# Ten instead of eight of 22 output steps by seven products, with one weight sum formed in DRAM by accumulating transfers

## The chip, the cores and the metric

The kernel runs on one core of one Trainium2 chip. The metric is the device time of one launch in microseconds (us). TensorE (PE) multiplies, VectorE (DVE) and ScalarE (ACT) prepare its operands and read its results, the queue of SyncE (SP) issues the weight loads, and GpSimd (POOL) issues the rest of the transfers through its own, software-driven queue. All transfers share the core's 16 DMA engines.

## What is computed

Two layers of a decoder on 256 tokens of width 2048, all in float32. Each layer is an attention block with a memory branch, followed by a convolutional feed-forward network, which holds most of the work:

```python
def conv_ffn(h, w_in, conv_w, conv_b, w_out):      # h [256, 2048], w_in [2048, 11264]
    u = h @ w_in
    up = jnp.pad(u, ((0, 0), (CONV_WIDTH - 1, 0), (0, 0)))
    c = conv_b
    for j in range(CONV_WIDTH):
        c = c + conv_w[j] * up[:, j:j + s]
    g, val = c[..., :D_FF], c[..., D_FF:]
    return (jax.nn.gelu(g, approximate=True) * val) @ w_out      # w_out [5632, 2048]
...
for layer in range(DEPTH):                          # DEPTH = 2
    mix = mla_mixer(...) if layer == 0 else diff_mixer(...)      # both end in concat(...) @ w_o
    x = x + rms_norm(mix, attn_norm_post)
    f = conv_ffn(rms_norm(x, ffn_norm_pre[layer]), ...)
    x = x + rms_norm(f, ffn_norm_post[layer])
```

The change concerns `@ w_out`, once in each layer.

## The kernel before

**Splitting.** Every float32 operand is held as two float32r parts, hi and lo with hi + lo = value, and a product is three matmuls (hi·hi, hi·lo, lo·hi). A weight block arrives as `w_raw`; ACT copies it to `w_hi` (the "split" of a step, `hi_ready`), DVE subtracts to get `w_lo` (`lo_ready`), then PE uses both (`step_used`). The program is one long row of numbered steps of two 128-row chunks by 512 columns (512 KB): first the memory products (`MEMA`, `MEMB`), the attention products (`QLAT` to `OA`), the feed-forward input `IN0` (176 steps in a loop of 11 turns) and output `OUT0`, then for layer 1 `SKV`, `BQ`, `OB`, `IN1`, `OUT1`. `w_raw`, `w_hi` and `w_lo` are rings of R = 4 slots: the load of a step waits until DVE has finished with the step four before it, and ACT's copy waits until PE has used that step. SP, ACT, DVE and PE each run their own list in order.

**The output stage.** hᵀ (5632 x 256, as `hT_hi`, `hT_lo`) stays on chip; W_out streams by. The 2048 columns are four tiles of 512, taken as two halves of two tiles. One tile has FSTEPS = 22 steps. A *plain* step is 2 chunks x 2 groups of 128 tokens x 3 = 12 matmuls of 512 columns into two PSUM banks. For the first PAIRS = 8 steps of a tile, the two tiles of a half are taken together as a *unit*: the four blocks of W (B11 and B21 of the left tile, B12 and B22 of the right one) and the four of h make a 2 x 2 block product, which is done by the seven products of Winograd's form of Strassen's scheme. That is 7 x 3 = 21 matmuls for what two plain steps do in 24. A unit is four entries of the list: `left` (6 matmuls), `corner` (3), `odd` (6), `even` (6). Three of its products need sums of weight blocks: DVE forms the odd sum (1024 columns, L2439) after `left`, and the even sum (512 columns twice, L2449 and L2452) after `corner`. The sums of h blocks ("forms") are made in the first PAIRS / 2 = 4 turns of the input loop and stay on chip in `s32_*` (in the room of x) and `s4_*`. At the end of a half, five DVE operations ("fold", L2905 to L2909, then L2913) gather the seven banks into tiles.

**The order of entries.** A table sets it by hand (`out_order`): a half has some plain steps first (`LEADS`), then the units with plain steps spread between them, then `REST` = 3 plain steps of the first tile (the fold hides behind them) and `TAILS` of the second. In the units' stretch the hi and lo rings have a fifth slot, `w5_*`, in room that xT has left.

**x and the other transfers.** x leaves for DRAM (`x_kept`) at the start of each input stage and comes back during the output stage, in four pieces of 512 KB (`x_returns`, L704), each after a pair of units of the second half; the fourth goes out when the last unit is done. `gain_o`, `gain_f`, `late_raw` and the memory keys and values (`km_kept`, `vm_kept`) go through POOL's queue as well.

Of the kernel before, what the change touches and what calls it, by code (L numbers as in the profile page):

```python
# [22 lines left out]
P = 128  # L23
# [26 lines left out]
R = 4  # L50
# [7 lines left out]
PAIRS = 8  # L58
# [7 lines left out]
LEADS = (CUT, 5)  # L66
REST, TAILS = 3, (4, 8)


def out_order():  # L70

    entries, raws = [], []

    def plain(tile, k):
        entries.append(("plain", tile, k, len(raws)))
        raws.append((tile, k, "entry", len(entries) - 1))

    def unit(half, p):
        r = len(raws)
        entries.extend((kind, 2 * half, p, r) for kind in ("left", "corner", "odd", "even"))  # L80
        for tile in (2 * half, 2 * half + 1):
            raws.append((tile, p, "unit", half * PAIRS + p))
# [27 lines left out]
WIDE = 100  # L110


def out_slots():

    slots, users, last = [], [], {k: k - R for k in range(R)}
    last[R] = -1
    for e in range(OSTEPS):
        slot = e % R
        turn = e - UNIT_STARTS[0]
        if 0 <= turn < WIDE:  # L120
            turn = turn % (R + 1)
            slot = (UNIT_STARTS[0] + turn - 1) % R if turn else R
        slots.append(slot)
        users.append(last[slot])
        last[slot] = e
    assert all(slots[e] == e % R for e in list(range(CUT)) + list(range(OSTEPS - R, OSTEPS)))
    assert EXTRA % R == 0 and OSTEPS % R == 0
    return slots, users


OUT_SLOTS, OUT_USERS = out_slots()
UNITS = 2 * PAIRS
PAIR_ENDS = [e + 1 for e in range(OUT_ENDS[1], OSTEPS) if OUT_ENTRIES[e][0] == "even"]
# [93 lines left out]
def raw_no(s):  # L227

    if s < OUT0:
        return s  # L230
    if s < SKV:
        return OUT0 + OUT_ENTRIES[s - OUT0][3]
    if s < OUT1:
        return s - EXTRA
    return OUT1 - EXTRA + OUT_ENTRIES[s - OUT1][3]
# [16 lines left out]
def program(nc, x_in, mem_in, positions, inv_freq, w, vec, out):  # L252

    with ExitStack() as ctx:
# [19 lines left out]
        raw_blocks = w_raw[:, :, :].rearrange("p r (a n) -> p (r a) n", a=2)  # L274
# [3 lines left out]
        s32_hi = at("s32_hi", [P, PAIRS // 2, 512], F32R, X0)  # L278
        s32_lo = at("s32_lo", [P, PAIRS // 2, 512], F32R, X0 + 8 * KB)
        s4_hi = at("s4_hi", [P, PAIRS // 2, 256], F32R, KVB0)  # L280
        s4_lo = at("s4_lo", [P, PAIRS // 2, 256], F32R, KVB0 + 4 * KB)
# [108 lines left out]
        def out_slot(e):  # L390


            slot = OUT_SLOTS[e]
            if slot == R:
                return w5_hi[:, :], w5_lo[:, :], w5_sum[:, :]
            return w_hi[:, slot], w_lo[:, slot], w_sum[:, slot]

        def unit_blocks(r):


            left, right = 2 * (r % R), 2 * ((r + 1) % R)
            outer = slice(left, left + 4, 3) if left < right else slice(right + 1, left + 1, 5)
            return (raw_blocks[:, outer, :], raw_blocks[:, left + 1], raw_blocks[:, right],
                    raw_blocks[:, right + 1])

        def odd_columns(r):


            low, high = slice(0, 512), slice(512, 1024)
            return (low, high) if r % R < R - 1 else (high, low)  # L410
# [32 lines left out]
        w_landed = [sem(f"w_landed{k}") for k in range(R)]  # L443
# [69 lines left out]
        odd_sums = sem("odd_sums")  # L513
# [7 lines left out]
        kv_spilled = sem("kv_spilled")  # L521
# [24 lines left out]
        def _(sp):  # L546
# [48 lines left out]
            def out_weights(s_out, name, layer):  # L595

                for r, (j, k, _, _) in enumerate(OUT_RAWS):
                    if r < R:
                        sp.wait_ge(lo_ready, s_out + r - R + 1)
                    elif OUT_RAWS[r - R][2] == "entry":  # L600
                        sp.wait_ge(lo_ready, s_out + OUT_RAWS[r - R][3] + 1)
                    else:
                        sp.wait_ge(unit_sums, layer * UNITS + OUT_RAWS[r - R][3] + 1)
                    sp.dma_start(w_raw[:, r % R, :].rearrange("p (c n) -> p c n", c=2),
                                 view[name][:, 2 * k:2 * k + 2, 512 * j:512 * (j + 1)])\
                        .then_inc(w_landed[r % R], 16)
# [48 lines left out]
        def _(pool):  # L655
# [17 lines left out]

            pool.wait_ge(lam_prod, 1)
            causal_rows(1)
            pool.wait_ge(o_lo, T0_B)
# [22 lines left out]
            def x_returns(s_out):  # L699


                for q in range(4):
                    pool.wait_ge(step_used, s_out + PAIR_ENDS[2 * q + 1])
                    pool.dma_start(x[:, :, 512 * q:512 * (q + 1)],  # L704
                                   x_kept[:, :, 512 * q:512 * (q + 1)]).then_inc(x_back, 16)

# [4 lines left out]
                .then_inc(kv_spilled, 16)  # L711
            pool.wait_ge(step_used, IN0 + 11)
            pool.dma_start(vm_kept, vm_b[:, :, :, :].rearrange("p u h n -> p (u h n)"))\
                .then_inc(kv_spilled, 16)
            gain_rows_of("ffn_post0", gain_f, OUT0)
            x_returns(OUT0)
            pool.wait_ge(step_used, SKV)
            causal_rows(2)
            pool.wait_ge(step_used, SKV + 2 * DSTEPS)
            pool.dma_start(kmT_b[:, :, :].rearrange("p h m -> p (h m)"), km_kept)\  # L720
# [2636 lines left out]
```

## Time and profile before

| | |
|---|---|
| median of 3 runs | 2162.6 us (2160.51 to 2163.26) |
| the profiled execution: its time, its span | 2161.88 us, 2159.7 us |
| PE busy in the span | 2147.9 us (99%) |
| DVE, ACT busy | 1620.6 us (75%), 1247.8 us (58%) |
| DMA | 416.68 MB, 193 GB/s on the mean |
| output stages | about 855 to 1084 us and 1924 to 2152 us from the span's start |

The span is what the profiler recorded of one execution; that execution's own time is 2.2 us longer and within the spread of the three runs. "Busy" counts the time in which an engine runs an instruction. Matmuls overlap, so a matmul's own duration is longer than the distance from one to the next; pace is read from a chain of them, as a stretch of time over their count.

### The profile page before, as it was taken

The numbers are of one execution on the slowest core, as the hardware profiler recorded it, in microseconds if no ns is written. First come the engines' busy times: TensorE is split into PE (matmuls) and PEld (weight loads), VectorE is DVE, ScalarE is ACT, GpSimd is POOL, SyncE is SP. The second block draws the span as 40 slices with busy tenths as digits, with TensorE's granted clock in tenths as the row PEclk, the third lists the DMA queues.
The fourth block names the chain that finished last, engine by engine and source line by source line (L and its number), as shares of the span: only waits on it lengthen the run. The fifth ranks groups of instructions, "written<-read, shape, count | busy, mean of one in ns | idle before, by whom it ended". The sixth has DMA issues, their size and how long they took to land.

```text
span 2159.7 us, 32620 instructions
## 1 busy us (share of the span) xinstructions
PE 2147.9 (99%) x11589; PEld 1861.3 (86%) x11589; DVE 1620.6 (75%) x2280; ACT 1247.8 (58%) x1764; POOL 20.1 (1%) x40
## 2 busy tenths in 40 slices
PE   9999999999999999999999999999999999999998
PEld 8989988888888888888888889888888888888887
DVE  5667756777777777988789877567778776779787
ACT  5755755666555555655565567466665555556554
POOL 0000000000000000000000000000000000000000
PEclk9999999999999999999999999999999999999999
DMA  8566266666656566666657644666655656566575
GB/s 285 177 186 182 92 199 195 209 196 191 188 179 204 181 196 201 197 221 211 223 167 225 198 158 127 194 192 196 196 183 179 201 175 204 178 207 209 195 229 189
DMA packets 204392, 416.68 MB, mean 193 GB/s; under 512 B 13245, under 2 KB 13623, under 8 KB 203535
## 3 DMA queue, kind: packets, MB, share of 16 engines
q1 hardware_dynamic: 200687, 400.29, 58.9%
q0 software_dynamic: 3616, 15.21, 2.0%
q8 instruction: 55, 0.90, 0.2%
q14 instruction: 34, 0.28, 0.0%
HBM read 408.11 MB, written 7.34 MB: 192 GB/s over the span
## 4 chain that ended last, share of the span: by engine, by line
PE 97%; DVE 1%; DMA 1%; ACT 0%; issue 0%; SPq 0%; DVEq 0%; ACTq 0%
PE ps L826 29%; PE ps L780 20%; PE ps L1320 20%; PE ps L834 15%; PE ps L864 4%; PE ps L874 3%; PE ps L1563 1%; PE ps L955 1%; PE ps L1466 0%; PE ps L1085 0%; DMA w_raw<-in_ffn_w_out 0%; PE ps L927 0%; PE ps L1020 0%; PE ps L1091 0%; PE ps L1116 0%; PE ps L1028 0%
## 5 line engine op out<-in xcount | busy, mean ns | idle before, releaser
L2504 DVE TENSOR_TENSOR w_lo<-w_raw,w_hi 128x1024 fp32r<-128x1024 f32 x450 | 541.4, 1221 | 256.1 <-ACT w_hi L1783 252.3
L826 PE MATMUL ps<-xT,w_hi 128*128 128x512 f32 x2752 | 657.6, 391 | 0.0
L1783 ACT ACTIVATE w_hi<-w_raw 128x1024 fp32r<-128x1024 f32 (+1 forms) x466 | 476.8, 1040 | 228.7 <-PE ps L780 85.3
L826 PEld LDWEIGHTS ps<-xT,w_hi 128*128 128x128 f32 x2752 | 505.4, 188 | 98.2 <-issue 0.4
L834 PEld LDWEIGHTS ps<-xT,w_lo 128*128 128x128 f32 x2752 | 353.1, 191 | 13.8 <-DVE w_lo L2504 0.4
L834 PE MATMUL ps<-xT,w_lo 128*128 128x256 f32 x2752 | 358.1, 283 | 0.0
L1320 PE MATMUL ps<-w_hi,hT_hi 128*128 128x512 f32 x576 | 224.4, 390 | 0.5 <-DVE w_lo L2428 0.5
L1320 PE MATMUL ps<-w_lo,hT_hi 128*128 128x512 f32 x576 | 224.1, 389 | 0.0
L1320 PE MATMUL ps<-w_hi,hT_lo 128*128 128x512 f32 x576 | 224.1, 389 | 0.0
L780 PE MATMUL ps<-w_hi,xT 128*128 128x512 f32 x640 | 203.3, 392 | 0.0
L2428 DVE TENSOR_TENSOR w_lo<-w_raw,w_hi 128x1024 fp32r<-128x1024 f32 x126 | 151.0, 1222 | 29.4 <-ACT w_hi L1737 25.3
L1737 ACT ACTIVATE w_hi<-w_raw 128x1024 fp32r<-128x1024 f32 x126 | 131.5, 1058 | 56.6 <-DMA w_raw<-in_ffn_w_out 40.3
L1779 ACT ACTIVATE w_hi<-w_raw,gcol 128x512 fp32r<-128x512 f32 x160 | 106.4, 717 | 62.6 <-PE ps L780 52.7
L780 PEld LDWEIGHTS ps<-w_hi,xT 128*128 128x128 f32 x640 | 120.2, 188 | 24.5
L1320 PEld LDWEIGHTS ps<-w_hi,hT_hi 128*128 128x128 f32 x576 | 108.1, 188 | 23.4 <-DVE w_lo L2428 0.9
L1320 PEld LDWEIGHTS ps<-w_hi,hT_lo 128*128 128x128 f32 x576 | 108.1, 188 | 22.6
L1320 PEld LDWEIGHTS ps<-w_lo,hT_hi 128*128 128x128 f32 x576 | 108.1, 188 | 22.4
L2491 DVE SCALAR_TENSOR_TENSOR w_lo<-w_raw,gcol,w_hi 128x512 fp32r<-128x512 f32 x160 | 111.9, 748 | 20.3 <-ACT w_hi L1779 19.6
L780 PE MATMUL ps<-w_lo,xT 128*128 128x512 f32 x320 | 124.7, 390 | 0.0
L1739 ACT ACTIVATE w_hi<-w_sum 128x1024 fp32r<-128x1024 f32 x64 | 68.0, 1063 | 86.1 <-DVE w_sum L2439 51.9
L780 PE MATMUL ps<-w_hi,xbT_hi 128*128 128x512 f32 x256 | 100.1, 391 | 0.0
L780 PE MATMUL ps<-w_hi,xbT_lo 128*128 128x512 f32 x256 | 99.7, 389 | 0.0
(343 smaller groups left out, 2746.0 us busy)
## 6 DMA issues: line engine op xcount, KB each, us to landing
w_raw<-in_ffn_w_in SPq DMA_DIRECT2D x352, 512.0 KB, 4.2
w_raw<-in_ffn_w_out SPq DMA_DIRECT2D x176, 512.0 KB, 4.8
w_raw<-in_shared_w_kv SPq DMA_DIRECT2D x48, 512.0 KB, 4.4
w_raw<-in_a_w_o SPq DMA_DIRECT2D x32, 512.0 KB, 4.8
w_raw<-in_b_w_in SPq DMA_DIRECT2D x32, 512.0 KB, 4.7
w_raw<-in_b_w_o SPq DMA_DIRECT2D x32, 512.0 KB, 4.3
w_raw<-in_a_w_mem_kv SPq DMA_DIRECT2D x16, 512.0 KB, 6.5
w_raw<-in_b_w_mem_kv SPq DMA_DIRECT2D x16, 512.0 KB, 4.0
```

The lines of the kernel that those rows point to most:

```text
L780: mm = nc.tensor.matmul(dst, st, mv, start=first and q == 0, stop=last and q == len(pairs) - 1, skip_group_check=True)
L826: mm = nc.tensor.matmul(ps[:, base + m4, :].rearrange("p (a n) -> p a n", a=2), w_hi[:, slot, cols], xT[:, :, 2 * k + c, :], start=k == c ...
L834: mm = nc.tensor.matmul(ps[:, base + m4, S:2 * S], w_lo[:, slot, cols], xT_hi[:, 2 * k + c, :], start=False, stop=stop and c == 1, skip_gr ...
L864: mm = nc.tensor.matmul(ps[:, bank, 256 * (h % 2):256 * (h % 2) + S], wk[:, P * h:P * (h + 1)], xk, start=bank not in begun, stop=False, s ...
L1320: mm = nc.tensor.matmul(ps[:, bank, :], st, mv, start=bank not in begun and q == 0, stop=False, skip_group_check=True)
L1737: a = nc.scalar.activation(hi, w_raw[:, r % R, :], ACT.Copy)
L1739: a = nc.scalar.activation(hi, sums_now, ACT.Copy)
L1779: a = nc.scalar.activation(w_hi[:, s % R, cols], w_raw[:, s % R, cols], ACT.Copy, scale=gcol[:, row:row + 1])
L1783: nc.scalar.activation(w_hi[:, s % R, 0:width], w_raw[:, s % R, 0:width], ACT.Copy)\
L2428: nc.vector.tensor_tensor(lo, w_raw[:, r % R, :], hi.bitcast(F32), ALU.subtract)\
L2491: d = nc.vector.scalar_tensor_tensor(out=w_lo[:, s % R, cols], in0=w_raw[:, s % R, cols], scalar=gcol[:, row:row + 1], in1=w_hi[:, s % R, ...
L2504: nc.vector.tensor_tensor(w_lo[:, s % R, :], w_raw[:, s % R, :], w_hi[:, s % R, :].bitcast(F32), ALU.subtract)\
```

## The change

It alters the output stages and what feeds them:

- `PAIRS` goes from 8 to 10, so a half has 10 units and 24 plain steps in place of 8 and 28. `LEADS` is (9, 4), `TAILS` (4, 7).
- The odd sum of a unit is no longer DVE's work. POOL forms it in DRAM (`odd_kept`), for two units at a time in four transfers of 512 KB (`odd_part`): two copies of blocks of W_out, and two transfers that add another block to what lies there (`accum_op`). There are 40 such transfers in a layer. Those of layer 0 go out from `MEMB` on, one in four steps (11), one behind each attention item (16), and two in each turn of the input loop (13); those of layer 1 one in four steps from `SKV` on (26), then in the input loop (14).
- A unit now has three loads: `left` 512 KB, `corner` 256 KB, and `odd` 512 KB from `odd_kept`.
- The forms of h go to DRAM (`s_kept`) in five turns of the input loop, and come back for each unit into one of two buffers (`s_now`, 384 KB a unit), when the unit two before it is done. PE waits for them at `corner`. The room of x thus holds two more raw slots (`x_raw`) and a sixth hi and lo slot (`w6_*`), used in the units' stretch ("turns"), until entry 117.
- x comes back from entry 117 on: four pieces, when 117, 118, 119 and 120 entries are done.

The core of the diff:

```diff
-PAIRS = 8
+PAIRS = 10
...
-LEADS = (CUT, 5)
-REST, TAILS = 3, (4, 8)
+LEADS, REST, TAILS = (CUT, 4), 3, (4, 7)
+EARLY_SUMS, MIDDLE_SUMS = 11, 26
...
+            def odd_part(layer, n):
+                g, part = n // 4, n % 4
+                half, p = 2 * g // PAIRS, 2 * g % PAIRS
+                chunk, tile, a, op = ((0, 0, 0, None), (1, 1, 1, None), (0, 1, 0, ALU.add),
+                                      (0, 1, 1, ALU.add))[part]
+                src = view[f"ffn_w_out{layer}"][:, 2 * p + chunk:2 * p + chunk + 3:2,
+                                                512 * (2 * half + tile):512 * (2 * half + tile + 1)]
+                dst = odd_kept[layer][2 * g:2 * g + 2, :, a, :].rearrange("u p n -> p u n")
+                if op is None:
+                    pool.dma_start(dst, src).then_inc(odd_copied, 16)
+                else:
+                    pool.wait_ge(odd_copied, 32 * (layer * PAIRS + g + 1))
+                    if part == 2 and layer + g > 0:
+                        pool.wait_ge(odd_summed, 32 * (layer * PAIRS + g))
+                    pool.dma_start(dst, src, accum_op=op).then_inc(odd_summed, 16)
...
-            pool.wait_ge(o_lo, T0_B)
+            for n in range(EARLY_SUMS):
+                pool.wait_ge(step_used, MEMB + 4 * (n + 1))
+                odd_part(0, n)
+            for n in range(T0_B):
+                pool.wait_ge(o_lo, n + 1)
+                odd_part(0, EARLY_SUMS + n)
             pool.dma_start(gain_o[:, :], vec["a_post"].partition_broadcast(P))\
                 .then_inc(gain_landed, 16)
...
-                    pool.wait_ge(step_used, s_out + PAIR_ENDS[2 * q + 1])
+                    pool.wait_ge(step_used, s_out + X_FREE + q)
                     pool.dma_start(x[:, :, 512 * q:512 * (q + 1)],
                                    x_kept[:, :, 512 * q:512 * (q + 1)]).then_inc(x_back, 16)
...
+            def forms_return(layer, s_out, no):
+                if no < 2:
+                    pool.wait_ge(s_stored, 32 + 16 * PAIRS * (layer + 1))
+                else:
+                    pool.wait_ge(step_used, s_out + UNIT_DONE[no - 2])
+                pool.dma_start(s_now[:, no % 2], s_kept[layer][no % PAIRS]).then_inc(s_landed[no % 2], 16)
...
                     if kind == "corner":
-                        return s(s4_hi, s4_lo, 0, a, 0)
+                        pe.wait_ge(s_landed[no % 2], 16 * (layer * PAIRS + no // 2 + 1))
+                        return s(2, a, 0)
...
-                if kind == "left":
-                    outer, _, b12, _ = unit_blocks(r)
-                    no = raw_no(s0) + r + 1
-                    dve.wait_ge(w_landed[no % R], 16 * (no // R + 1))
-                    dve.wait_ge(step_used, s0 + OUT_USERS[e + 2] + 1)
-                    nc.vector.tensor_tensor(
-                        out_slot(e + 2)[2].rearrange("p (a n) -> p a n", a=2), outer,
-                        b12.unsqueeze(1).to_broadcast([P, 2, 512]), ALU.add)\
-                        .then_inc(odd_sums, 1)
```

DVE's list at the first units of layer 0. Before, the first unit and the plain step behind it (the names are those of the text, with buffer numbers):

```order
L2428 TENSOR_TENSOR w5_lo_56<-w_raw_51,w5_hi_55 128x1024
L2439 TENSOR_TENSOR w_sum_54<-w_raw_51 128x1024
L2424 TENSOR_TENSOR w_lo_53<-w_raw_51,w_hi_52 128x512
L2449 TENSOR_TENSOR w_sum_54<-w_sum_54,w_raw_51 128x512
L2452 TENSOR_TENSOR w_sum_54<-w_sum_54,w_raw_51 128x512
L2431 TENSOR_TENSOR w_lo_53<-w_sum_54,w_hi_52 128x1024 x2
L2428 TENSOR_TENSOR w_lo_53<-w_raw_51,w_hi_52 128x1024
```

Of the change, the same first unit and the `left` and `corner` of the next:

```order
L2532 TENSOR_TENSOR w5_lo_56<-x_raw_58,w5_hi_55 128x1024
L2514 TENSOR_TENSOR w6_lo_60<-x_raw_58,w6_hi_59 128x512
L2525 TENSOR_TENSOR w_sum_54<-w_raw_51,x_raw_58 128x512
L2528 TENSOR_TENSOR w_sum_54<-w_sum_54,x_raw_58 128x512
L2532 TENSOR_TENSOR w_lo_53<-w_raw_51,w_hi_52 128x1024
L2532 TENSOR_TENSOR w_lo_53<-w_sum_54,w_hi_52 128x1024
L2532 TENSOR_TENSOR w_lo_53<-w_raw_51,w_hi_52 128x1024
L2514 TENSOR_TENSOR w_lo_53<-w_raw_51,w_hi_52 128x512
```

The 1024-column sum is gone, the lo part of `odd` is taken straight from a raw slot, and the second unit follows with no plain step between.

POOL's list from the last accumulating transfer of layer 0 to the end of its output stage. Of the change:

```order
L717 DMA odd_kept<-in_ffn_w_out 128x2x512 x2
L785 DMA s_now<-s_kept 128x768 x2
L738 DMA gain_f<-in_ffn_norm_post 128x2048
L785 DMA s_now<-s_kept 128x768 x18
L754 DMA x<-x_kept 128x2x512 x4
```

Before, this place had two rows:

```order
L688 DMA gain_f<-in_ffn_norm_post 128x2048
L704 DMA x<-x_kept 128x2x512 x4
```

Twenty returns of forms were added ahead of x, on the same queue.

SP's list in the last entries of the output stage of the change (from the odd sum of the last unit but one to the end of layer 1); before, this was an unbroken row of 512 KB loads:

```order
L632 DMA x_raw_58<-odd_kept1 128x1024
L632 DMA w_raw_51<-in_ffn_w_out 128x2x512 x3
L632 DMA w_raw_51<-in_ffn_w_out 128x512
L632 DMA w_raw_51<-odd_kept1 128x1024
L632 DMA w_raw_51<-in_ffn_w_out 128x2x512 x10
```

The `128x512` row is a `corner`, the `odd_kept1` rows are the ready sums; the last ten loads feed the plain steps 118 to 127, on the four slots of `w_raw` alone.

## Rows read from the trace of the kernel before

**Rows 1.** The page: busy time of each engine, share, instructions.

```profile
PE 2147.9 (99%) x11589; PEld 1861.3 (86%) x11589; DVE 1620.6 (75%) x2280; ACT 1247.8 (58%) x1764; POOL 20.1 (1%) x40
```

**Rows 2.** What PE waited for: us in total, times, longest.

```profile
PE ps L864 <- ACT w_hi L1764: 1.3, 1, 1.3
...
PE ps L1320 <- DVE w_lo L2428: 0.5, 1, 0.5
```

**Rows 3.** Chain that ended last: start us, us; layer 0's end, then layer 1's output.

```profile
1054.29 9.12 DMA w_raw<-in_ffn_w_out
...
1069.71 1.14 DVE w_lo L2428
...
1070.90 12.58 PE ps L1320 x54
...
1923.79 228.67 PE ps L1320 x1008
```

**Rows 4.** Windows: start:end, length, busy us (count) by engine, PEclk, DMA share, GB/s.

```profile
core 0: us, PE busy (x) PEld busy (x) DVE busy (x) ACT busy (x) POOL busy (x), PEclk, DMA share, GB/s
376.00:855.00 479.00, 478.99 (x2756) 423.23 (x2755) 355.63 (x433) 274.96 (x322) 2.44 (x4) 1.00 0.62 193
881.00:946.00 65.00, 65.00 (x288) 53.83 (x287) 60.44 (x62) 38.44 (x40) 0.00 (x0) 1.00 0.65 210
```

**Rows 5.** Groups of DVE: line, tiles, shapes, count | busy us, mean ns | idle before.

```profile
L2428 DVE TENSOR_TENSOR w_lo<-w_raw,w_hi 128x1024 fp32r<-128x1024 f32 x126 | 151.0, 1222 | 29.4 <-ACT w_hi L1737 25.3
L2439 DVE TENSOR_TENSOR w_sum<-w_raw 128x1024 f32<-128x1024 f32 x32 | 39.0, 1219 | 4.6 <-PE ps L1320 4.6
L2452 DVE TENSOR_TENSOR w_sum<-w_sum,w_raw 128x512 f32<-128x512 f32 x32 | 22.1, 692 | 1.1
L2449 DVE TENSOR_TENSOR w_sum<-w_sum,w_raw 128x512 f32<-128x512 f32 x32 | 22.0, 688 | 5.3 <-PE ps L1320 5.3
L2424 DVE TENSOR_TENSOR w_lo<-w_raw,w_hi 128x512 fp32r<-128x512 f32 x32 | 21.9, 685 | 0.0
L3135 DVE TENSOR_TENSOR scratch<-scratch 128x256 f32<-128x256 f32 x8 | 3.4, 425 | 0.3
```

**Rows 6.** Loads of weights in the input stage of layer 0, 380 to 850 us.

```profile
L552 SPq DMA_DIRECT2D w_raw<-in_ffn_w_in x164: 372/373/548, 381.7 to 838.1; - x164
...
DMA to landing us min/median/max: 3.4/4.2/7.4
```

**Rows 7.** Loads in the output stage issued from 1054 to 1056 us.

```profile
L604 SPq DMA_DIRECT2D w_raw<-in_ffn_w_out x2: 368/368/368, 1054.3 to 1055.4; - x2
...
DMA to landing us min/median/max: 9.1/9.2/9.3
```

**Rows 8.** Returns of x, the whole trace.

```profile
L704 POOL DMA_DIRECT2D x<-x_kept x8: 704/718/728, 995.9 to 2122.8; - x8
...
DMA to landing us min/median/max: 4.2/6.3/8.8
```

**Rows 9.** Short windows, columns as in rows 4, in which the DMA share is near 1.

```profile
12.00:15.00 3.00, 3.00 (x21) 2.69 (x20) 2.03 (x3) 2.75 (x6) 0.00 (x0) 1.00 1.00 391
...
1056.00:1058.00 2.00, 2.00 (x10) 1.69 (x9) 1.93 (x4) 0.60 (x1) 0.00 (x0) 1.00 0.98 254
...
1062.00:1064.00 2.00, 2.00 (x11) 1.65 (x10) 0.00 (x0) 0.57 (x1) 0.00 (x0) 1.00 0.98 331
...
1076.00:1078.00 2.00, 2.00 (x10) 1.65 (x10) 1.23 (x1) 0.17 (x1) 0.00 (x0) 1.00 1.00 351
```

**Rows 10.** Input stage: ACT's timeline, then two pieces of the chain.

```profile
607.81 1.06 ACT L1783 ACTIVATE w_hi<-w_raw 128x1024 fp32r<-128x1024 f32 x1 [1.70 <-PE ps L834]
...
603.17 3.65 PE ps L826 x16
606.82 1.91 PE ps L834 x16
```

**Rows 11.** POOL's timeline: gain_o, and the last return of x.

```profile
280.44 0.68 POOL L677 DMA_DIRECT2D gain_o<-in_a_attn_norm_post  x1 [215.55 <-DVE xT L2812]
...
1054.41 0.72 POOL L704 DMA_DIRECT2D x<-x_kept  x1 [19.69 <-PE ps L1320]
```

**Rows 12.** Use of gain_o: durations in ns, first and last start.

```profile
L2932 DVE TENSOR_TENSOR y_o<-ps,gain_o x3: 1219/1224/1225, 294.3 to 338.0; 128x1024 f32<-128x1024 f32 x3
```

More of the change, by code:

```diff
@@ L62, with load @@
 FJ = F // 512
-LEADS = (CUT, 5)
-REST, TAILS = 3, (4, 8)
+LEADS, REST, TAILS = (CUT, 4), 3, (4, 7)
+EARLY_SUMS, MIDDLE_SUMS = 11, 26
 def out_order():
     entries, raws = [], []
+    def load(kind, tile, k, e, unit_no=None):
+        raws.append((kind, tile, k, e, unit_no))
+        return len(raws) - 1
     def plain(tile, k):
-        entries.append(("plain", tile, k, len(raws)))
-        raws.append((tile, k, "entry", len(entries) - 1))
+        e = len(entries)
+        entries.append(("plain", tile, k, load("plain", tile, k, e)))
     def unit(half, p):
[L79 to L82, printed above, removed]
+        e, no = len(entries), half * PAIRS + p
+        for n, kind in enumerate(("left", "corner", "odd")):
+            entries.append((kind, 2 * half, p, load(kind, 2 * half, p, e + n, no)))
+        entries.append(("even", 2 * half, p, None))
     ends, unit_ends, unit_starts = [], [], []
@@ L87, in out_order @@
         first, second = ([(2 * half + j, k) for k in ks] for j in range(2))
-        between = first[LEADS[half]:-REST] + second[:-TAILS[half]]
-        for step in first[:LEADS[half]]:
+        steps = first[:-REST] + second[:-TAILS[half]]
+        between = steps[LEADS[half]:]
+        for step in steps[:LEADS[half]]:
             plain(*step)
@@ L109, with turns @@
 EXTRA = OSTEPS - len(OUT_RAWS)
[L110 to L122, printed above, removed]
+SLOTS = R + 2
+def turns(n, last_wide):
+    wide = (last_wide - CUT) // 12 * 12
+    slots, users, uses, last = [], [], [], {k: k - R for k in range(R)}
+    count = [0] * SLOTS
+    for e in range(n):
+        slot, turn = e % R, e - CUT
+        if 0 <= turn < wide:
+            slot = R + turn % SLOTS if turn % SLOTS < 2 else (CUT + turn % SLOTS - 2) % R
+        count[slot] += 1
         slots.append(slot)
-        users.append(last[slot])
+        users.append(last.get(slot))
+        uses.append(count[slot])
         last[slot] = e
[L126 to L131, printed above, removed]
+    assert all(slots[e] == e % R for e in list(range(CUT)) + list(range(n - R, n)))
+    assert n % R == 0
+    return slots, users, uses, CUT + wide, n // R - count[0]
+OUT_SLOTS, OUT_USERS, _, SLOTS_END, _ = turns(OSTEPS, OSTEPS - R)
+RAW_SLOTS, RAW_USERS, RAW_USES, RAWS_END, DIVERTED = turns(len(OUT_RAWS), len(OUT_RAWS) - R)
+X_FREE = max(SLOTS_END, max(raw[3] for raw in OUT_RAWS[:RAWS_END]) + 1)
 UNITS = 2 * PAIRS
-PAIR_ENDS = [e + 1 for e in range(OUT_ENDS[1], OSTEPS) if OUT_ENTRIES[e][0] == "even"]
+UNIT_DONE = [e + 1 for e in range(OSTEPS) if OUT_ENTRIES[e][0] == "even"]
 MEMA, MEMA_T = 0, 0
@@ L393, in out_slot, with raw_slot @@
             slot = OUT_SLOTS[e]
-            if slot == R:
-                return w5_hi[:, :], w5_lo[:, :], w5_sum[:, :]
+            if slot >= R:
+                return ((w5_hi[:, :], w5_lo[:, :], w5_sum[:, :]),
+                        (w6_hi[:, :], w6_lo[:, :], w6_sum[:, :]))[slot - R]
             return w_hi[:, slot], w_lo[:, slot], w_sum[:, slot]
[L398 to L410, printed above, removed]
+        def raw_slot(r):
+            slot = RAW_SLOTS[r]
+            return w_raw[:, slot] if slot < R else x_raw[:, slot - R]
         def mem_gain_row(s):
@@ L512, in program @@
         s_lo = sem("s_lo")
-        odd_sums = sem("odd_sums")
+        odd_copied = sem("odd_copied")
+        odd_summed = sem("odd_summed")
+        s_stored = sem("s_stored")
+        s_landed = [sem(f"s_landed{k}") for k in range(2)]
         even_sum = sem("even_sum")
@@ L1374, in out_product @@
                         pe.wait_ge(lo_ready, s0 + e + 1)
-                        if half == 0 and (j, k) == (0, FSTEPS - 2):
+                        if half == 0 and kind == "plain" and k == FSTEPS - 2:
                             pe.wait_ge(h_lo, h_done)
                         mm = plain(e, k, 2 - 2 * (j % 2), range(TT)) if kind == "plain" else \
-                            unit(e, kind, k, r)
+                            unit(e, kind, k, half * PAIRS + k)
                         mm.then_inc(step_used, 1)
```

200 lines of the change are left out of this document (120 added, 80 removed).

## Prediction

> **What bounds the kernel now.** I read the page's busy times first: PE is busy for 2147.9 of 2159.7 us, with DVE at 75% [rows 1]. Then the waits of PE itself: the longest of the whole program is 1.3 us, and in the output stages there is a single one, of 0.5 us [rows 2]. Then the chain that ended last: the output stage of layer 1 is one piece, 1008 matmuls in 228.67 us with nothing between them [rows 3], which is 226.9 ns a matmul. The clock is at full, 1.00, in all windows [rows 4]. So PE's own work is the bound, and only two things can move the time: the number of matmuls, and a new wait of PE. DVE, ACT and the transfers matter only if one of them comes late.
>
> **Matmuls.** Before, a layer's output has 56 plain steps x 12 + 16 units x 21 = 1008. After: 48 x 12 + 20 x 21 = 996. Twelve fewer in a layer, 24 in all, at 226.9 ns: **-5.44 us**. Nothing of this hides behind anything, since PE has no slack.
>
> **DVE in the output stage.** An odd sum took 1219 ns, 32 of them 39.0 us [rows 5]; all go. A unit then costs DVE 3 x 1.222 + 0.685 + 0.688 + 0.692 = 5.73 us, against 6.95 before. The densest stretch is the first half, entries 9 to 56. Before: 8 units and 12 plain steps, 312 matmuls or 70.8 us of PE, and 8 x 6.95 + 12 x 1.22 = 70.3 us of DVE. After: 10 units and 8 plain steps, 306 matmuls or 69.4 us, and 57.3 + 9.8 = 67.1 us of DVE. So DVE's share falls from 99% to 97% by these durations. They overlap by a little: measured it was 60.44 of 65 us, or 93% [rows 4], and PE didn't wait there. DVE thus gets looser, not tighter, and earns nothing, since it was hidden already: 0.
>
> **One more turn of forms.** Five turns of the input loop make them in place of four: four operations of 0.425 us and a lo part of about 1.1 us (0.685 + 0.42), some 2.8 us of DVE a layer. DVE is busy for 355.63 of 479 us in that stage [rows 4]: 0. POOL stores them in the next turn 13 steps in, and ACT needs the buffer some 7 steps later. A step is half of 3.65 + 1.91 us [rows 10], 2.78 us, so 19 us stand against a landing of 4.2 to 8.8 us for POOL's 512 KB transfers [rows 8]: 0.
>
> **Traffic of the units.** In the first half's stretch the loads are 10 x 1280 KB + 8 x 512 KB, and the forms 10 x 384 KB: 21.2 MB in 69.4 us, 306 GB/s. In the second (10 units, 10 plain steps, 74.9 us) it is 297. Before, the same sum gives 207 GB/s for the first stretch, and the window shows 210 [rows 4], so the sum can be trusted. What can the engines move? With their share near 1 the windows show 254, 331, 351 and 391 GB/s [rows 9]. The 391 had rows of 4 KB, as the new odd loads have; 331 and 351 are loads of 2 KB rows, as most of the rest; 254 was a mix with a return of x. I take 330 to 350: 306 is nine tenths of it. Loads will take longer, 6 us perhaps where they took under 5. Six raw slots turn over in 6 x 69.4 / 38 = 11 us, of which DVE and ACT hold one for about 3, so a landing of 8 us is still covered. I take 0 here; the bounds are 0 (331 and up) and what 254 would give, in the rivals. The Trainium skill (HBM Reference, Specifications) gives about 358 GB/s as a core's share of HBM. By that the demand fits, and the sum stays; the windows agree, with 351 at a share of 1.00.
>
> **The wait for forms.** PE now waits at `corner`. The return is issued when the unit two before is done. The shortest case is the third unit: one unit, one plain step and a `left`, 21 + 12 + 6 = 39 matmuls or 8.85 us; the others have 51 matmuls, 11.6 us. Returns of x, a third bigger, landed in 4.2 to 8.8 us [rows 8]. Cover is enough for all but perhaps two in the program: 0 to 1 us, I take 0.2.
>
> **The end of each output stage.** Here is the one place where a transfer already reached PE. The last piece of x was issued at 1054.41 [rows 11]. The loads issued beside it at 1054.3 and 1055.4 took 9.1 to 9.3 us [rows 7], against 4.2 for a common one [rows 6]. The first of them stands in the chain [rows 3]: the fold's last part and the next tile's squares are queued behind its split, and so the split of the third plain step of the tail ended at 1070.86 and PE, due 0.5 us sooner, waited. After the change, the pieces of x go out at entries 117 to 120, within 6 to 7 us, where before three of the four were long gone. Bounds: below 0 more (the load that matters is the second in SP's queue, and the pieces behind it come too late to pass it). Above: 1.5 MB more in the same stretch at 254 GB/s is 6 us; half of it lies behind the load that matters, which leaves 3, in each of two layers. I take the lower end, with 0.1 to 0.2 a layer, since POOL spaces the pieces by a step each: **+0.3**.
>
> **The 80 transfers of sums.** Loads in the input stage take 4.2 us [rows 6]. ACT's copy there waits for PE to free its slot, not for data [rows 10]; PE has then three steps more ready, 8.35 us, less 2.3 for the split itself. So a load may come 6 us late, taking 10.2 us, before PE stands. One 512 KB piece of x cost a load 5 us. An accumulating transfer isn't in this trace. Below it costs what a copy does (hidden); above, twice the piece of x, since it reads two operands: 4.2 + 10 = 14 us, 4 over. I take it as nearer the copy, as a step-by-step spacing of 11 to 14 us leaves the engines (share 0.62 [rows 4]) time to clear each: 0. In the attention stage POOL may run some 4 us late (it waits for a copy issued one item before), and `gain_o` goes out at about 284.5, not at 280.44 [rows 11]. With a landing of 4.2 to 8.8 us [rows 8] it is there by 293.3, and its first use is at 294.3 [rows 12]: hidden.
>
> **Sum.** -5.44 + 0.2 + 0.3 = -4.9 us. The profiled execution took 2161.88 us (span 2159.7), the median of the runs is 2162.6, 0.7 above. From the median: 2157.7 us. A measurement of this kernel can tell about 0.2%, 4.3 us, from no change, so this lies just beyond it; below 2158.3 I count as faster, above 2166.9 as slower.
>
> **Rivals.**
> *A, the units' stretch is bound by transfers* (the other side). The four stretches hold 40 units and 36 plain steps. The gain is used up when a unit's turn grows by 5.44 / 40 = 0.14 us, that is when the engines move less than about 300 GB/s of this mix. For it speaks the window with 254 GB/s beside a return from POOL's queue [rows 9]; the forms return by that queue all through the stretch. Against it, the higher windows, and that only 18% of the bytes are such. At 280 GB/s a turn takes 7.6 us in place of 6.94: +0.6 x 40 = +25, 2182 us. Chance 0.13.
> *B, x comes back in a bunch.* The mechanism above at its upper end: +3 us in each layer, 2163.5 us, no change. The Trainium skill (DMA: Bandwidth & Descriptors, Queues, rings and completion order) says that each DMA engine takes its queues in turn, packet by packet. By that rule x's queue, kept full, takes half of what each engine moves, which is this rival; the trace agrees in part, 9.1 us beside one piece. Chance 0.22.
> *C, the accumulating transfers hold up the loads.* At the upper bound above, 40 accumulations over by 4 us are +160 us; at a tenth of that excess +16, 2174 us. Chance 0.07.
> *D, the change doesn't bring its 24 matmuls' time,* because other small stalls (attention of layer 1, the third unit) take 2 to 4 us: 2160 to 2162. Chance 0.06.
> The forecast itself has 0.52: 2156.8 to 2159.0, nearly all of it faster.
>
> **How the numbers follow.** Faster: the forecast's share below 2158.3, 0.50, and a little of D, 0.52. Same: B, D and the forecast's rest, with a part of A and C that stays small, 0.29. Slower: the rest, 0.19. The range goes from 2156 (no stall at all, and a run 1 us low) to 2174, which takes in B, D and the smaller forms of A and C. The likeliest case alone has 2156.5 to 2159.5.
>
> **What would show it.** PE: 996 matmuls in one piece of the chain, about 226 us, in layer 1. Waits of PE in the output stages under 1 us. DVE's busy time in the output stages about 13 us down (a layer has 8 x 1.22 less in plain steps and 20 x 5.73 - 16 x 6.95 = 3.4 more in units, -6.4). Loads in the stretch of units at 5 to 7 us, DMA share there 0.85 to 0.95 with 300 GB/s. If PE waits for `w_lo` behind a DMA all through the units, A holds; if only within 15 us of the stage's end, B; if in the input loop, C. Wrong it would be most of all if the mix of queues moves less than 300 GB/s.

## The result, and the profile after

| | median | runs | ratio to before |
|---|---|---|---|
| before | 2161.61 us (2160.51 to 2163.26) | 6 | |
| changed | 2176.57 us (2173.12 to 2178.24) | 6 | 1.0066, 95% interval 1.0053 to 1.0079 |

The change made the kernel slower by 15 us, where 2157.7 us, 4.9 us faster, was forecast. The profiled execution of the changed kernel took 2178.24 us with a span of 2176.5, 16.8 us more than the span of before.

The page of the changed kernel (columns as in [rows 1]), then what PE waited for (as in [rows 2]):

```profile
PE 2148.5 (99%) x11565; PEld 1859.8 (85%) x11565; DVE 1612.9 (74%) x2282; ACT 1262.3 (58%) x1778; POOL 133.3 (6%) x180
```

```profile
PE ps L874 <- DVE w_lo L2584: 11.7, 1, 11.7
PE ps L1414 <- DVE w_lo L2532: 2.1, 3, 0.8
PE ps L1414 <- DVE ps L2989: 2.1, 2, 1.2
```

The first line says that PE has its 24 matmuls fewer (11565 against 11589) and yet is busy for 0.6 us longer; the second, that it has one wait of 11.7 us that wasn't there. L874 is the product of the attention output projection (`OA`), far ahead of both output stages. The chain of work through that place, start us and us:

```profile
251.81 5.03 DMA odd_kept<-in_ffn_w_out
...
257.37 2.33 POOL odd_kept L717 x2
259.70 0.57 POOL odd_kept L712
260.27 10.15 DMA odd_kept<-in_ffn_w_out
...
270.95 2.12 POOL odd_kept L717 x2
273.07 11.73 DMA odd_kept<-in_ffn_w_out
...
285.33 2.12 POOL odd_kept L717 x2
287.45 16.00 DMA odd_kept<-in_ffn_w_out
...
303.97 0.71 POOL odd_kept L717
304.68 8.40 DMA gain_o<-in_a_attn_norm_post
313.11 1.23 DVE y_o L3012
314.33 1.14 DVE w_lo L2584
315.52 29.58 PE ps L874 x119
```

Read it from the bottom. PE waits for a lo part; DVE made it late because `y_o`, which multiplies by `gain_o`, stands ahead of it in DVE's list; `gain_o` landed at 313.1, since POOL issued it at 304.68 and not at 280.44 as in [rows 11]; and POOL was late because, three times in a row, it stood at a wait for copies (L712) that took 10.15, 11.73 and 16.00 us to land. The same from POOL's and DVE's timelines, where the bracket gives the idle time and what ended it:

```profile
285.33 2.33 POOL L717 DMA_DIRECT2D odd_kept<-in_ffn_w_out  x2 [10.64 <-DMA odd_kept<-in_ffn_w_out]
286.75 2.33 POOL L712 DMA_DIRECT2D odd_kept<-in_ffn_w_out  x2
303.97 1.16 POOL L717 DMA_DIRECT2D odd_kept<-in_ffn_w_out  x1 [14.90 <-DMA odd_kept<-in_ffn_w_out]
304.68 1.05 POOL L727 DMA_DIRECT2D gain_o<-in_a_attn_norm_post  x1
```

```profile
313.11 1.23 DVE L3012 TENSOR_TENSOR y_o<-ps,gain_o 128x1024 f32<-128x1024 f32 x1 [17.74 <-DMA gain_o<-in_a_attn_norm_post]
```

`y_o` starts 18.8 us later than in [rows 12]; PE had work in hand for some 7 of them. Four transfers go out together each time (two that add, two copies), and yet the landings grow from 10.15 to 16.00 us; what made the last the longest isn't shown, but the loads of the projection's weights had begun beside it. Windows of the changed kernel, columns as in [rows 4]:

```profile
300.00:310.00 10.00, 3.83 (x17) 2.83 (x16) 0.00 (x0) 3.17 (x3) 3.06 (x4) 0.84 0.71 173
310.00:320.00 10.00, 4.48 (x11) 3.55 (x12) 5.76 (x5) 0.00 (x0) 0.00 (x0) 0.50 0.60 211
320.00:330.00 10.00, 10.00 (x45) 8.25 (x44) 2.39 (x2) 3.01 (x3) 0.00 (x0) 0.98 0.59 194
...
376.00:855.00 479.00, 478.97 (x2757) 422.29 (x2756) 362.48 (x443) 281.75 (x336) 24.70 (x29) 1.00 0.70 216
897.00:966.00 69.00, 69.00 (x306) 57.17 (x305) 63.31 (x66) 44.49 (x48) 4.76 (x9) 1.00 0.89 307
```

The wait costs more than itself. After it PE runs at a granted clock of 0.50 (1.2 of 2.4 GHz), so the chain's last piece has 119 matmuls in 29.58 us where 119 x 0.2269 is 27.0: 2.6 us more. 11.7 + 2.6 = 14.3 us.

Where the 16.8 us lie is seen from PE's first and last matmul of each output stage in its timeline (those of before start at 855.35 and 1085.34, and at 1923.63 and 2152.06):

```profile
872.43 0.39 PE L1414 MATMUL ps<-w_hi,hT_hi 128*128 128x512 f32 x1
...
1101.42 0.39 PE L1414 MATMUL ps<-w_hi,hT_lo 128*128 128x512 f32 x1
...
1939.63 0.39 PE L1414 MATMUL ps<-w_hi,hT_hi 128*128 128x512 f32 x1
...
2168.81 0.39 PE L1414 MATMUL ps<-w_hi,hT_lo 128*128 128x512 f32 x1
```

- Ahead of layer 0's output stage: +17.1. Of these 14.3 are the place above; 2.4 had come up by 105 us. PE was busy for only 0.26 us between 7 and 9 us (1.04 before); behind that its granted clock fell to 0.50 between 10 and 12 us, and was 0.91 over the first 20 us (1.00 before).
- Layer 0's output stage: 228.99 against 229.99, -1.0. Layer 1's: 229.18 against 228.43, +0.75.
- Between the stages -0.1, and behind them +0.05.

So there are two misses: the projection, and the output stages, which together should have been 5.44 us shorter and were 0.25. The chain at the end of layer 0's output stage shows the second; layer 1 has the same rows, with a landing of 6.15 us for the load, and one more short wait for a lo part:

```profile
1059.85 6.59 PE ps L1414 x29
...
1066.53 0.70 DVE w_sum L2525
...
1067.95 1.15 DVE w_lo L2532
1069.11 5.86 DMA w_raw<-in_ffn_w_out
1074.99 1.07 ACT w_hi L1831
...
1076.08 1.23 DVE w_lo L2532
...
1079.99 1.24 DVE ps L2989
...
1081.28 8.45 PE ps L1414 x36
```

The last unit's even sum waits for PE, then everything behind it runs in a row (lo part, the next load into the slot that it frees, split, lo part, the five operations of the fold), and PE waits for the fold. Nothing waits so in the units' stretch: in the window 897 to 966, its dense first half, PE is busy for 69.00 of 69 us at a share of 0.89 and 307 GB/s.

### The profile page after: what moved, and what is told of

Same layout as the page of the kernel before. It is cut to its first block, busy times and chain, and to the rows that moved or that the text cites. A ratio compares the mean times of both kernels' runs of the same rounds, so it can differ in the third digit from the quotient of the medians.

```text
span 2176.5 us, 32947 instructions
## 1 busy us (share of the span) xinstructions
PE 2148.5 (99%) x11565; PEld 1859.8 (85%) x11565; DVE 1612.9 (74%) x2282; ACT 1262.3 (58%) x1778; POOL 133.3 (6%) x180
## 3 DMA queue, kind: packets, MB, share of 16 engines
q0 software_dynamic: 41696, 80.75, 15.1%
## 4 chain that ended last, share of the span: by engine, by line
PE 93%; DMA 4%; DVE 2%; ACT 1%; POOL 0%; issue 0%; SPq 0%; DVEq 0%; POOLq 0%; ACTq 0%
PE ps L920 29%; PE ps L1414 19%; PE ps L874 18%; PE ps L928 15%; PE ps L958 4%; PE ps L968 3%; DMA odd_kept<-in_ffn_w_out 2%; PE ps L1656 1%; PE ps L1049 1%; DMA w_raw<-in_a_w_in 1%; DMA w_raw<-in_ffn_w_out 1%; PE ps L1559 0%; PE ps L1021 0%; DMA gain_o<-in_a_attn_norm_post 0%; POOL odd_kept L717 0%; PE ps L1210 0%
## 5 line engine op out<-in xcount | busy, mean ns | idle before, releaser
L2584 DVE TENSOR_TENSOR w_lo<-w_raw,w_hi 128x1024 fp32r<-128x1024 f32 x450 | 540.9, 1221 | 259.6 <-ACT w_hi L1875 256.5
L874 PE MATMUL ps<-w_hi,xT 128*128 128x512 f32 x640 | 205.2, 395 | 11.7 <-DVE w_lo L2584 11.7
L1414 PE MATMUL ps<-w_hi,hT_hi 128*128 128x512 f32 x544 | 212.5, 391 | 4.3 <-DVE w_lo L2532 2.1
L1414 PE MATMUL ps<-w_hi,hT_lo 128*128 128x512 f32 x544 | 211.7, 389 | 0.0
L1414 PE MATMUL ps<-w_lo,hT_hi 128*128 128x512 f32 x544 | 211.7, 389 | 0.0
L2532 DVE TENSOR_TENSOR w_lo<-w_raw,w_hi 128x1024 fp32r<-128x1024 f32 x116 | 140.3, 1221 | 24.0 <-ACT w_hi L1831 23.3
L874 PEld LDWEIGHTS ps<-w_hi,xT 128*128 128x128 f32 x640 | 121.3, 190 | 37.0 <-DVE w_lo L2584 12.1
L1831 ACT ACTIVATE w_hi<-w_raw 128x1024 fp32r<-128x1024 f32 x116 | 121.1, 1056 | 46.6 <-DMA w_raw<-in_ffn_w_out 24.2
L1414 PEld LDWEIGHTS ps<-w_hi,hT_hi 128*128 128x128 f32 x544 | 102.1, 188 | 27.9 <-DVE w_lo L2532 4.0
L874 PE MATMUL ps<-w_lo,xT 128*128 128x512 f32 x320 | 125.7, 393 | 0.0
L1414 PEld LDWEIGHTS ps<-w_hi,hT_lo 128*128 128x128 f32 x544 | 102.1, 188 | 21.3
L1414 PEld LDWEIGHTS ps<-w_lo,hT_hi 128*128 128x128 f32 x544 | 102.2, 188 | 21.0
L874 PE MATMUL ps<-w_hi,xbT_hi 128*128 128x512 f32 x256 | 100.1, 391 | 0.0
L874 PE MATMUL ps<-w_hi,xbT_lo 128*128 128x512 f32 x256 | 99.6, 389 | 0.0
L874 PE MATMUL ps<-w_lo,xbT_hi 128*128 128x512 f32 x256 | 99.6, 389 | 0.0
```

Source lines behind the costliest of these rows:

```text
L874: mm = nc.tensor.matmul(dst, st, mv, start=first and q == 0, stop=last and q == len(pairs) - 1, skip_group_check=True)
L1414: mm = nc.tensor.matmul(ps[:, bank, :], st, mv, start=bank not in begun and q == 0, stop=False, skip_group_check=True)
L1831: a = nc.scalar.activation(hi, src, ACT.Copy)
L2532: nc.vector.tensor_tensor(lo, src, hi.bitcast(F32), ALU.subtract)\
L2584: nc.vector.tensor_tensor(w_lo[:, s % R, :], w_raw[:, s % R, :], w_hi[:, s % R, :].bitcast(F32), ALU.subtract)\
```

## The experiments

Times of before in the batches of these runs were 2161.55 to 2161.71 us; a ratio is always to before. The names are numbered in the order in which they ran.

**e1_gain_first: `gain_o` ahead of the last copies, and these spread over the projection.**

```diff
+ITEM_SUMS = 11
...
             for n in range(T0_B):
                 pool.wait_ge(o_lo, n + 1)
-                odd_part(0, EARLY_SUMS + n)
+                if n < ITEM_SUMS:
+                    odd_part(0, EARLY_SUMS + n)
...
+            for n in range(ITEM_SUMS, T0_B):
+                pool.wait_ge(step_used, OA + 8 + 4 * (n - ITEM_SUMS))
+                odd_part(0, EARLY_SUMS + n)
```

> The 16 sum transfers behind the attention items become 11; gain_o and late_raw follow at once when the attention is done, and the other five go out later, one in four steps of the products with w_o. Number and size of transfers stay. Theory 1 (gain_o was queued behind waits for bunched copies on GpSimd's queue, DVE stood before it for 17.7 us, PE for 11.7 us and ran at half clock after it): the first product with w_o gets about 14 us back, 2162 to 2163 us. Theory 2 (the traffic as such slows the loads all over): within 3 us of the change, 2174 or more.

Measured: 2160.95 us (2159.63 to 2163.33, 10 runs), ratio 0.9997, interval 0.9987 to 1.0006. POOL's timeline of this kernel:

```profile
281.09 0.58 POOL L729 DMA_DIRECT2D gain_o<-in_a_attn_norm_post  x1 [8.48 <-DVE xT L2897]
```

PE's wait in the projection is gone, and with it 15.6 us. The rest of the result is this: without that place the change is worth nothing, 2161.0 against 2161.7. Its first and last matmuls stand 229.13 and 228.43 us apart in the output stages, 0.9 us shorter than before in the sum of both, where 5.44 were forecast.

**e2_tails8: eight plain steps, not seven, of the second tile behind the second half's units.**

```diff
-LEADS, REST, TAILS = (CUT, 4), 3, (4, 7)
+LEADS, REST, TAILS = (CUT, 4), 3, (4, 8)
```

> One plain step less between the units of the second half and one more behind them, so that the last unit ends at entry 117, inside the stretch with six slots. Theory S (the last unit falls on the narrow ring, its even sum waits for a slot, and with it the loads behind it): the two stalls of about 1.7 and 3.5 us at the ends of the output stages go, 2171 to 2173 us. Theory X (the four returns of x in a bunch make those loads late): they stay, 2175 to 2178 us.

Measured: 2173.51 us (2170.72 to 2174.39, 4 runs), ratio 1.0056, interval 1.0039 to 1.0073: 3.1 us below the changed kernel. The chain of this kernel has layer 1's output in one piece, as in [rows 3]:

```profile
1934.99 225.94 PE ps L1414 x996
```

That is 226.8 ns a matmul and no wait, 2.7 us less than 228.67. From first to last matmul the output stages are 226.99 and 225.70 us, 5.5 us less than those of the changed kernel together; this profiled execution is the fastest of the four, and the medians differ by 3.1. With one step more behind it, the last unit ends with entry 116 and falls inside the stretch with the six-slot ring (`turns`). With TAILS (4, 7) the wide ring ends one entry short of it: entry 117, the last unit's `even`, takes slot 1 of four, which entry 113 had, where in the wide ring it would follow an entry six back, and its sum can't be formed until PE is through with entry 113. The wait of 11.7 us in the projection stayed as it was, so the two places are apart.

**e3_copies: the second transfers copy in place of adding.** The odd sums are then one addend alone.

```diff
-                    pool.dma_start(dst, src, accum_op=op).then_inc(odd_summed, 16)
+                    pool.dma_start(dst, src).then_inc(odd_summed, 16)
```

> The 40 accumulating transfers of a layer half become plain copies of the same size at the same places with the same waits (the odd sums are then wrong: one block instead of a sum). Theory A (accumulating is what is dear: it reads two operands): the landings of these transfers fall below 7 us, gain_o goes out 8 us or more earlier and the time falls to 2166 to 2170 us. Theory C (a transfer from DRAM to DRAM is as dear, whatever it does): less than 3 us of difference.

Measured: 2161.61 us (2160.92 to 2164.46, 10 runs), ratio 1.0001, interval 0.9991 to 1.0011. DVE still waits for `gain_o`, but not long enough to reach PE:

```profile
297.92 1.22 DVE L3012 TENSOR_TENSOR y_o<-ps,gain_o 128x1024 f32<-128x1024 f32 x1 [5.03 <-DMA gain_o<-in_a_attn_norm_post]
```

The order of the list is that of the changed kernel, with the same bytes and waits; 15 us went with the adding alone. POOL still bunches its transfers and waits for copies, the longest for 11.7 us. The transfers of the window from 240 to 310 us: the queue's packets, MB and share of the 16 engines' time, then issues with the median us to landing. First the changed kernel, then this one:

```profile
q0 software_dynamic: 3344, 8.55, 56.6%
q1 hardware_dynamic: 2479, 4.77, 19.3%
...
odd_kept<-in_ffn_w_out POOLq DMA_DIRECT2D x16, 512.0 KB, 9.4
w_raw<-in_a_w_o SPq DMA_DIRECT2D x8, 512.0 KB, 9.6
```

```profile
q0 software_dynamic: 2608, 9.96, 46.3%
q1 hardware_dynamic: 3497, 6.75, 29.5%
...
odd_kept<-in_ffn_w_out POOLq DMA_DIRECT2D x16, 512.0 KB, 6.5
w_raw<-in_a_w_o SPq DMA_DIRECT2D x13, 512.0 KB, 5.3
```

**e4_no_sums: no transfers of sums at all.** The sums aren't formed; the load of `odd` takes two blocks of W_out.

```diff
             def odd_part(layer, n):
+                return
...
-                        src = odd_kept[layer][no].rearrange("p a n -> p (a n)")
+                        dst = dst.rearrange("p (c n) -> p c n", c=2)
+                        src = view[name][:, 2 * k:2 * k + 2, 512 * (j + 1):512 * (j + 2)]
```

> No sum transfers at all: the odd load reads two blocks of w_out instead of the stored sum (the odd products are then wrong). It bounds all that the 80 transfers cost. Theory 1: what they cost is the wait for gain_o and next to nothing else, so this is within 2 us of the run with gain_o first, 2160 to 2163 us. Theory 2: lower than that run by more than 3 us.

Measured: 2160.14 us (2158.86 to 2161.93, 10 runs), ratio 0.9993, interval 0.9984 to 1.0003. Only 0.8 us below e1_gain_first, within what the runs can tell: apart from the place before the projection, 80 accumulating and copying transfers are hidden. The output stages still have their waits, 1.6 us for the fold and 1.4 for the lo part (1.6 and 1.8 in e1_gain_first), so those don't come from the sums.

**e8_gain_by_sp: `gain_o` alone goes out by SP's queue; the sums stay as they were.**

```diff
+                if j == 1:
+                    sp.wait_ge(o_lo, T0_B)
+                    sp.dma_start(gain_o[:, :], vec["a_post"].partition_broadcast(P))\
+                        .then_inc(gain_first, 16)
```

> The changed kernel with all 16 item transfers where they are, but gain_o issued by SyncE's queue when attention is done. GpSimd stays late, and late_raw with it. Theory 1 (only the place behind GpSimd's waits held up gain_o): it goes out at about 281 us, lands by 291 to 295, and the 14 us are back, 2161 to 2163 us. Theory 2 (the four transfers then in flight take the engines, whoever issues gain_o): it lands after 300 us, and 3 us or more stay, 2165 to 2172 us.

Measured: 2162.31 us (2161.15 to 2172.68, 10 runs), ratio 1.0006, interval 0.9997 to 1.0016. The median says that `gain_o`'s place in POOL's list is the cause of nearly all of it. But two of the ten took 2169.78 and 2172.68, and the profiled one is the latter. Its chain there:

```profile
286.08 15.08 DMA w_raw<-in_a_w_o
302.27 1.18 DVE w_lo L2587
...
305.88 9.00 DMA w_raw<-in_a_w_o
```

Here the loads of the projection's own weights took 15 and 9 us beside the bunch of sums, and PE waited 6.6 us in three pieces. (Another 2.2 us of this execution had come up by 105 us, with the granted clock of the first 20 us at 0.91 here too.) So the bunch has a second way to reach PE, which `gain_o`'s wait hid in the changed kernel. e1_gain_first thins the bunch too, and none of its ten runs went above 2163.33.

**e7_x_spread: as e1_gain_first, but x comes back every other entry.**

```diff
-                    pool.wait_ge(step_used, s_out + X_FREE + q)
+                    pool.wait_ge(step_used, s_out + X_FREE + 2 * q)
```

> As the run with gain_o first (last unit on the narrow ring), but the four returns of x go out two entries apart instead of one. Theory S (the narrow ring's slot is what PE waits for at the ends): no difference from 2160.95, within 1 us, with the waits of PE at the ends still there. Theory X (the bunched returns slow the loads that matter): the waits go and it is 2157 to 2159 us.

Measured: 2159.46 us (2158.8 to 2164.01, 10 runs), ratio 0.9993, interval 0.9983 to 1.0002. 1.5 us below e1_gain_first, and not clearly apart from it by the runs; in the profiles its two output stages are 1.3 us shorter. PE's waits for the fold and the lo part are still 1.6 and 1.4 us.

**e5_gain_tails: e1_gain_first and TAILS (4, 8) together.**

> Both orders together: gain_o and late_raw ahead of the last five sum transfers, and the last unit inside the stretch with six slots. In the run with the last unit moved, PE waited for nothing in the output stages and they took 226.5 and 225.3 us. If both causes are what they seem, the time is that of the matmuls alone: the 2160.95 us of the run with gain_o first less the 3.4 us that PE waited in its output stages, 2157 to 2158.5 us, and faster than the kernel before beyond the measurement. If the two stalls are one and the same (late traffic), nothing more is gained: 2160 or more.

Measured: 2157.41 us (2156.05 to 2161.16, 11 runs), ratio 0.998, interval 0.9971 to 0.9989. It beats both kernels. All that PE still waits for in the output stages:

```profile
PE ps L1419 <- DVE ps L2994: 1.5, 2, 0.9
```

**e6_eight_pairs: e1_gain_first with eight pairs, LEADS (9, 5) and TAILS (4, 12).** All else of the change stays.

```diff
-PAIRS = 10
+PAIRS = 8
-LEADS, REST, TAILS = (CUT, 4), 3, (4, 7)
+LEADS, REST, TAILS = (CUT, 5), 3, (4, 12)
```

> The same with PAIRS = 8 (LEADS 9 and 5, TAILS 4 and 12, so that the last unit is inside the wide stretch too): the new structure, with sums in DRAM, forms from DRAM and six slots, without the two extra units a half. 24 matmuls more at 226.9 ns. Theory P (PE is the only bound, the matmul term of 5.4 us is right): 5.4 us above the run with ten, 2162.5 to 2164 us, with no wait of PE. Theory D (the traffic of ten units costs part of it again): less than 4 us above.

Measured: 2164.19 us (2162.83 to 2166.72, 10 runs), ratio 1.0011, interval 1.0002 to 1.0021. Layer 1's output in its chain:

```profile
1927.72 228.49 PE ps L1419 x1008
```

6.8 us above e5_gain_tails, where 24 matmuls are 5.44. The profiled executions don't put it all in the output stages: of the 8.3 us between them 3.2 lie ahead of the first output stage and 1.7 between the two, where loads of `shared_w_kv` took 10.6, 7.0 and 9.5 us in the chain, with short waits of PE that I didn't follow. The stages themselves differ by 3.4 us (229.15 and 228.26 us here), and e5_gain_tails still waits for 1.5 us in them, which this kernel doesn't.

**e9_twelve_pairs: e5_gain_tails with twelve pairs.**

```diff
-PAIRS = 10
+PAIRS = 12
```

> The kernel with gain_o ahead of the last copies and an eighth plain step at the end of a half, but with twelve of 22 steps of a tile in units: 984 matmuls a layer's output in place of 996, 24 fewer in the program. Theory (PE is the only bound, the units' stretch has transfer capacity left): 5.44 us below the same kernel with ten, so 2152 us, output stages 224.1 us each, no wait of PE in the first half's units. Rival (the first half's stretch becomes transfer-bound): twelve units and four plain steps behind nine leading ones ask for 12 x 1664 KB + 4 x 512 KB = 22.5 MB in 300 matmuls or 68.1 us, 331 GB/s; then PE waits for w_lo behind loads in that stretch, the DMA share is near 1.00, and the time is 2157 us or above.

Measured: 2159.98 us (2158.6 to 2162.86, 11 runs), ratio 0.9992, interval 0.9983 to 1.0001: 2.6 us above e5_gain_tails. Neither view was right. In the window from 881 to 950 us the engines have a share of 0.93 and move 306 GB/s, short of full, and PE waits for something else, the forms:

```profile
PE ps L1419 <- DMA s_now<-s_kept: 3.8, 4, 1.6
```

```profile
892.95 11.18 PE ps L1419 x48
904.12 0.64 issue
904.76 6.31 DMA s_now<-s_kept
```

With no plain step between two units, the return that is issued when a unit is done has 27 matmuls, 6.1 us, before it is wanted, and takes 0.64 + 6.31. Traffic may have a part in it: this return and the next one in the chain took 6.3 and 6.8 us to land, where the median of e5_gain_tails is 4.9. The output stages are 227.8 and 226.4 us from first to last matmul, against 227.3 and 226.7 of e5_gain_tails, so the 5.44 us were used up there; 2.6 us more had come up before 857 us, and I don't know from what.

**e10_both_spread: e5_gain_tails with x every other entry.**

> The kernel with gain_o ahead of the last copies and an eighth plain step at the end of a half (2157.4 us), and with the pieces of x coming back every other entry instead of every entry. Theory (the bunch of x costs nothing once the last unit is on the wide ring): 2157.4, within 0.7 us. Rival (the bunch of x still delays loads near the stage's end): 1 to 2 us less, 2156, and the last wait of PE for the fold, 1.5 us in two, is shorter.

Measured: 2156.85 us (2155.35 to 2162.33, 11 runs), ratio 0.9982, interval 0.9973 to 0.9991. The fastest median, but 0.6 us from e5_gain_tails is less than its runs can tell. The last waits for the fold fell from 1.5 to 0.4 us. The output stages are 227.15 and 225.93 us, 0.9 us less than those of e5_gain_tails together.

## Why the prediction was wrong

**The step that failed** is the last of *The 80 transfers of sums*: "POOL may run some 4 us late (it waits for a copy issued one item before), and `gain_o` goes out at about 284.5", and so is hidden. It went out at 304.68. The mechanism was seen, its size was wrong by 20 us, for two reasons. First, I let POOL wait for one landing; but a wait that makes POOL late also makes the next transfers go out together, two adding ones and two copies within 4 us, and these then land later still: 5.0 us for a copy issued 2 us behind the one before it, then 10.2, 11.7 and 16.0 us with four together. That each delay feeds the next is my reading of this order; no run spaces the four apart and changes nothing else. Second, I took an adding transfer "as nearer the copy", and the copy from the returns of x, at 4.2 to 8.8 us. With copies alone the median is 6.5, and `gain_o` is out at 290.4 (e3_copies): 6 us later than I said, and still harmless. With adding it is 9.4 and the slack is used up. The text even had the number, 14 us as an upper bound, but applied it to loads in the input stage and not to POOL's own wait. And the price of being late was never asked: `gain_o` had 1 us of slack by my own sum (293.3 against 294.3), and behind `y_o` stood the lo parts on which PE lives.

**Matmuls, -5.44: right.** 996 in 225.94 us (e2_tails8), 1008 in 228.49 (e6_eight_pairs), and e2's two output stages are 5.7 us shorter than those of before. That e6 and e5 are 6.8 us apart as whole kernels is in part other waits and shows less.

**The end of each output stage, +0.3: too low, and for another cause.** The changed kernel's stages lost 5.2 us against the matmul count. By the medians TAILS (4, 8) gives back 3.1 (e2_tails8) or 3.5 (e5 against e1), by the output stages of the profiles 5.5 or 3.5. What I had not seen is the ring: entry 117 on a four-slot ring whose predecessor PE still uses. I had costed only the returns of x. They cost 1.5 us (e7 against e1) or 0.6 (e10 against e5), at the edge of what can be measured. The load in the chain took 5.86 us (6.15 in layer 1) against a common 5.3; it was issued 2 us ahead of the first piece. The next four loads, beside the pieces, did take 7.6 to 9.0 us (8.9 to 9.7 in layer 1), but PE didn't wait for them. So rival B's slow loads are there, and its +3 us a layer is not. The Trainium skill (DMA: Bandwidth & Descriptors, Queues, rings and completion order) has the engines take their queues in turn; the 3 us a layer that I derived from it do not show here.

**DVE in the output stage, 0: right as a cost.** Its busy time fell by 9.5 us (from 389.5 in 855 to 1085 and 1924 to 2152, to 380.0 in the stages after), where 13 was forecast.

**Traffic of the units, 0: right, and rival A refuted.** 307 GB/s at a share of 0.89 in the densest 69 us with PE never waiting, and loads with a median of 5.9 us there, all as forecast; e5_gain_tails has the same 307 at 0.89. Even twelve pairs did not fill the engines. One reading in that term was wrong: the windows were said to agree with 358 GB/s, by the one of 351, but [rows 9] also has 391 at a share of 1.00, so they show no ceiling there.

**The wait for forms, +0.2, and the turn of forms, 0: right** for ten pairs, where no wait for `s_now` shows. For twelve it is this wait that binds.

**Rival C had the right actor in the wrong place.** It priced accumulating transfers that hold up loads in the input loop, at 2174 us. In the input loop PE is busy for 478.97 of 479 us. The damage was done in the attention stage, through POOL's list, and (e8_gain_by_sp) at times through the projection's loads. That its 2174 is close to 2176.57 is chance.

**Rival D** had other small stalls eat up the gain. That is what e1_gain_first shows with its 2160.95 us, but not from D's places: between the output stages the changed kernel takes 838.21 us where before took 838.29, and the third unit doesn't wait. It is the last unit's slot again.

The account: 15.6 us from `gain_o` behind the sums (e1), 3.5 from the last unit's slot (e5 against e1), some 1 from x (e7, e10), the sums otherwise 0.8 (e4 against e1), and -5.4 of matmuls. 15.6 + 3.5 + 1 + 0.8 - 5.4 is 15.5, and 15.0 was measured. e5_gain_tails, with the two misses mended, takes 2157.41 us where 2157.7 was forecast. What stays open is why PE had so little work between 7 and 9 us in two of the profiled executions (the changed kernel's and e8_gain_by_sp's), ahead of the clock's fall there. It is 2.4 us of the changed kernel's profile. In how many of its six executions it happened isn't known, so a part of the 15.6 us may be this, as the place in the projection took 14.3 in the profile.

## What to carry to other kernels

When a queue that issues transfers in order gets new work with waits in it, list what stands behind that work and give each its slack; a transfer with 1 us of slack (`gain_o`, 1 MB) belongs ahead of 512 KB transfers that nobody needs for 600 us. Don't price a chain of waits by one landing: a queue that comes late issues its backlog at once, and the backlog lands later. And when a ring changes its width at an entry, look at the entries at the seam: one plain step more behind the last unit was worth 3 us or more.

## What was not expected of the hardware

- A transfer that adds to what lies in DRAM loads the engines more than a copy. In the window from 240 to 310 us POOL's queue moved 8.55 MB in 56.6% of the engines' time with adding, 216 GB/s at a full share (8.55 MB / 70 us / 0.566), and 9.96 MB in 46.3% with copies, 307 GB/s. Loads beside them took 9.6 and 5.3 us (medians). The MB are the profile's count, which is the same for a transfer that adds and for a copy. Over the whole program the queue has the same 80.75 MB in both, with 41696 packets and a share of 15.1%, against 36576 and 11.8%. POOL spends 1.16 us to issue one that adds and 0.69 for a copy (x40 each).
- After 11.7 us without a matmul PE's granted clock was 0.50 when it took up work (0.50 in the window 316 to 320 us, 0.88 in 320 to 322, 1.00 behind it), at a price of 2.6 us on top of the wait. The Trainium skill (TensorE: Matmul & The Clock Gate, What's actually happening) says that the clock has two states, 1.2 and 2.4 GHz, and that work releases the throttle; the trace agrees, with 0.50 and 1.00.
